# Four RMS norms: the last chunk's squares are added on VectorE before the partition sums, and one more chunk of products goes first in two of them

## The reference

```python
def rmsnorm(x, g):
    xf = x.astype(F32)
    y = xf * lax.rsqrt(jnp.mean(xf * xf, axis=-1, keepdims=True) + EPS)
    return (y * g.astype(F32)).astype(x.dtype)
...
x = x + g1 * (ox @ mla_w_o[j])
...
x = x + g2 * conv_ffn(modulate(rmsnorm(x, norm_ffn_g[i]), sh2, sc2), *ffn)
...
x = x + merged @ w_out[l]
...
return _rmsnorm(x, final_norm_g)
```

## Time and profile before

| | us |
|---|---|
| median of 3 runs | 1647.57 |
| lowest, highest | 1644.97, 1647.64 |
| the profiled execution, span | 1645.5 |

### The profile page before, as it was taken

One profiled execution on the slowest core, in us unless ns is written; L12 is line 12 of the kernel. 1 busy time (PEld: TensorE's weight loads), 2 busy tenths in 40 slices (PEclk: granted clock), 3 DMA queues, 4 the chain that ended last, 5 costly groups with the idle time before them and its releaser, 6 DMA issues.

```text
span 1645.5 us, 24018 instructions
## 1 busy us (share of the span) xinstructions
PE 1633.9 (99%) x8950; PEld 1364.2 (83%) x8950; DVE 1043.6 (63%) x1537; ACT 571.0 (35%) x1017; POOL 1026.5 (62%) x656
## 2 busy tenths in 40 slices
PE   9999999999999999999999999999999999999998
PEld 7887778798888888889887798888888898888887
DVE  3567777677877865635487566655558359746173
ACT  3467777633233232203344243222222121123111
POOL 3455766656666766575579456666676645567663
PEclk9999999999999999999999999999999999999999
DMA  9234335232269863435322233344434253223332
GB/s 371 87 90 129 111 106 165 79 93 96 89 211 320 298 225 103 141 137 172 120 90 65 77 99 102 125 156 140 153 106 143 97 214 120 65 84 103 91 101 90
DMA packets 59095, 220.61 MB, mean 134 GB/s; under 512 B 6849, under 2 KB 9153, under 8 KB 55682
## 3 DMA queue, kind: packets, MB, share of 16 engines
q1 hardware_dynamic: 53826, 204.96, 38.2%
q10 hardware_dynamic: 5184, 14.49, 2.3%
HBM read 201.07 MB, written 14.16 MB: 131 GB/s over the span
## 4 chain that ended last, share of the span: by engine, by line
PE 95%; DVE 4%; ACT 0%; issue 0%; DMA 0%; DVEq 0%; SPq 0%; ACTq 0%
PE PS L2444 28%; PE PS L2446 28%; PE PS L2445 28%; PE PS L2821 3%; PE PS L2783 2%; PE PS L1012 1%; PE PS L2430 1%; PE PS L1785 1%; PE PS L2595 1%; DVE SC L3572 0%; DVE WA L1990 0%; PE PS L1791 0%; DVE MR L3522 0%; PE PS L2720 0%; PE PS L2721 0%
## 5 line engine op out<-in xcount | busy, mean ns | idle before, releaser
L2354 POOL TENSOR_TENSOR WL<-RAW,WH 128x1024 fp32r<-128x1024 f32 (+3 forms) x211 | 542.8, 2572 | 17.6
L2444 PE MATMUL PS<-HH,WH 128*128 128x512 f32 (+1 forms) x1340 | 507.5, 379 | 0.0
L2446 PE MATMUL PS<-HH,WL 128*128 128x512 f32 (+1 forms) x1340 | 502.9, 375 | 0.0
L2445 PE MATMUL PS<-HL,WH 128*128 128x512 f32 (+1 forms) x1340 | 502.9, 375 | 0.0
L2351 POOL TENSOR_SCALAR WH<-RAW 128x1024 fp32r<-128x1024 f32 (+3 forms) x211 | 239.4, 1134 | 287.8 <-PE PS L2446 276.5
L2444 PEld LDWEIGHTS PS<-HH,WH 128*128 128x128 f32 x1340 | 252.2, 188 | 50.7 <-issue 6.2
L2446 PEld LDWEIGHTS PS<-HH,WL 128*128 128x128 f32 x1340 | 252.2, 188 | 45.9
L2445 PEld LDWEIGHTS PS<-HL,WH 128*128 128x128 f32 x1340 | 252.3, 188 | 43.9
L2379 POOL TENSOR_SCALAR PR<-PR,SC 128x768 f32<-128x768 f32 x47 | 107.3, 2292 | 66.7 <-DVE SC L3579 66.3
L2444 PE MATMUL PS<-HIDH,WH 128*128 128x512 f32 (+1 forms) x396 | 145.3, 367 | 0.0
L2445 PE MATMUL PS<-HIDL,WH 128*128 128x512 f32 (+1 forms) x396 | 144.8, 366 | 0.0
(11 more groups left out here) (532 smaller groups left out, 2894.6 us busy)
## 6 DMA issues: line engine op xcount, KB each, us to landing
RAW<-in_wup SPq DMA_DIRECT2D x88, 512.0 KB, 3.6
MRF<-in_modw SPq DMA_DIRECT2D x52, 512.0 KB, 4.8
RAW<-in_wdn SPq DMA_DIRECT2D x32, 704.0 KB, 4.1
MR<-in_modw SPq DMA_DIRECT2D x28, 512.0 KB, 3.6
RAW<-in_whin SPq DMA_DIRECT2D x24, 512.0 KB, 3.5
MK<-in_modk SPq DMA_DIRECT2D x8, 1024.0 KB, 10.9
RAW<-in_wo SPq DMA_DIRECT2D x8, 512.0 KB, 4.2
hy_hs<-HST ACTq DMA_DIRECT2D x4, 1024.0 KB, 4.0
```

The source lines that it names most:

```text
L2354: pool.tensor_tensor(WL[s][:, 0:n], raw[:, 0:n], WH[s][:, 0:n].bitcast(F32), ALU.subtract).then_inc(tile_split, 1)
L2444: pe.matmul(out, wh, xh, start=first, stop=False)
L2445: pe.matmul(out, wh, xl, start=False, stop=False)
L2446: return pe.matmul(out, wl, xh, start=False, stop=last)
```

## The change

In the norms `ffn0`, `hy`, `ffn1` and `n2` VectorE adds the squares of chunk 7 to the running sum (`last_add`, half by half; `n2` has two additions a half), and TensorE sums only SSQ (and SSQ2) over the partitions, behind one wait on `sq_add` in place of the waits on `radd` and `rsq`. `last_add(0)` stands ahead of `half_scale(name, 0)`, `last_add(1)` behind `scaled(2, 0)`. In `ffn0` and `ffn1` the last chunk of tile 6 half 1 goes ahead of the sum, with its `tile_done`. `fin2` stays as it was.

```diff
@@ -2473,19 +2473,21 @@
             def stat_half(name, h):
 
                 n = HALVES[name][1]
-                pe.wait_ge(S["radd"], 7 * n + 6 + h)
-                pe.wait_ge(S["rsq"], 10 * n + 8 + 2 * h)
+                if name == "fin2":
+                    pe.wait_ge(S["radd"], 7 * n + 6 + h)
+                    pe.wait_ge(S["rsq"], 10 * n + 8 + 2 * h)
+                    terms = (SSQ, SQ[1])
+                else:
+                    pe.wait_ge(S["sq_add"], 2 + 2 * n + h)
+                    terms = (SSQ,)
                 for b in (2 * h, 2 * h + 1):
                     r = slice(P * b, P * b + P)
-                    pe.matmul(PS[:, 4, b:b + 1], SSQ[:, r], ONES[:, 0:1], start=True, stop=False)
-                    m = pe.matmul(PS[:, 4, b:b + 1], SQ[1][:, r], ONES[:, 0:1], start=False, stop=True)
+                    for term in terms:
+                        m = pe.matmul(PS[:, 4, b:b + 1], term[:, r], ONES[:, 0:1], start=term is SSQ, stop=term is terms[-1])
                 if name == "n2":
-                    pe.wait_ge(S["radd2"], 6)
-                    pe.wait_ge(S["rsq2"], 8 + h)
                     for b in (2 * h, 2 * h + 1):
                         r = slice(P * b, P * b + P)
-                        pe.matmul(PS[:, 4, 4 + b:5 + b], SSQ2[:, r], ONES[:, 0:1], start=True, stop=False)
-                        m = pe.matmul(PS[:, 4, 4 + b:5 + b], SQ2[1][:, r], ONES[:, 0:1], start=False, stop=True)
+                        m = pe.matmul(PS[:, 4, 4 + b:5 + b], SSQ2[:, r], ONES[:, 0:1], start=True, stop=True)
                 m.then_inc(S["hstat"], 1)
 
             LAST_AT = {2: PS[:, 4, 2:3], 3: PS[:, 5, 2:3]}
@@ -2531,7 +2533,10 @@
                     pe.wait_ge(S["resid"], RBASE[stage] + 6)
                     pe.wait_ge(tile_split, tile_at(stage, 7) + 1)
                     part(7, 0, 0, 0, kn).then_inc(S["half"], 1)
-                    part(6, 0, 1, late, kn - 1)
+                    if name == "fin2":
+                        part(6, 0, 1, late, kn - 1)
+                    else:
+                        part(6, 0, 1, late, kn).then_inc(tile_done, 1)
                 else:
                     pe.wait_ge(S["resid"], RBASE[stage] + 6)
                     pe.wait_ge(tile_split, tile_at(stage, 7, 2, 0) + 1)
@@ -2542,7 +2547,7 @@
                     part(7, 1, 0, 0, kn).then_inc(S["half"], 2)
                     part(7, 0, 1, late, kn).then_inc(tile_done, 1)
                 stat_half(name, 0)
-                if tiles == 1:
+                if name == "fin2":
                     part(6, 0, 1, kn - 1, kn).then_inc(tile_done, 1)
                 ready = {"ffn0": 3, "hy": 4, "ffn1": 3, "n2": 6, "fin2": 3}[name]
                 part(7, tiles - 1, 1, 0, ready)
@@ -3762,6 +3767,17 @@
                                                        ALU.subtract)
                     ins.then_inc(S["hnl"], 1)
 
+                def last_add(h):
+                    dve.wait_ge(S["rsq"], 10 * n + 8 + 2 * h)
+                    dve.wait_ge(S["radd"], 7 * n + 6 + h)
+                    ins = dve.tensor_tensor(SSQ[:, tok(h)], SSQ[:, tok(h)], SQ[1][:, tok(h)], ALU.add)
+                    if name == "n2":
+                        dve.wait_ge(S["rsq2"], 8 + h)
+                        dve.wait_ge(S["radd2"], 6)
+                        ins = dve.tensor_tensor(SSQ2[:, tok(h)], SSQ2[:, tok(h)], SQ2[1][:, tok(h)], ALU.add)
+                    ins.then_inc(S["sq_add"], 1)
+
+                last_add(0)
                 half_scale(name, 0)
                 if name in SPLIT:
                     middle()
@@ -3775,6 +3791,8 @@
                     if k >= 4:
                         low(k - 2, 0)
                     scaled(k, 0)
+                    if k == 2:
+                        last_add(1)
                     if k == 5:
                         half_scale(name, 1)
                 for k in range(2):
```

## The result

The changed kernel takes 1649.2 us (median of 18 runs), the one before 1647.0 in the same session; the ratio is 1.0019 with a 95% interval of 1.0012 to 1.0025, so 3.1 us slower (2.0 to 4.1), just inside 0.2%. The forecast was +2.4. The fastest executions of each, 1647.4 and 1644.6, are 2.8 apart. The profiled execution has a span of 1649.5 us, 4.0 more than that of before.

What follows compares the result with a forecast made beforehand. TensorE, busy 99%, bounds the kernel, but VectorE sets the pace at k=2 to 4 of the norms. -0.2 (`ffn0`, `ffn1`) + 0.2 (`hy`) + 2.35 (`n2`) = +2.4 us on 1647.57 gives 1649.9 us, range 1646.8 to 1654.6.

Steps and rivals of the forecast that it cites:

- TensorE's side: In the four norms, 4.5 us of matmuls removed over two halves; wins before k=4 count only if `low(4)` comes earlier.
- The additions: Ten VectorE additions of 128x256 in the four norms, 0.42 us each, with bounds 0.35 and 0.70.
- `ffn0`, `ffn1`: In these two norms the second addition starts 0.13 us ahead of L2354; `low(2)` 0.1 us earlier in each, together -0.2 us.
- `hy`: In this norm the first half gains 0.15 us, L2354 is 0.08 behind the second addition, and `low(2)` is 0.2 us later.
- The order of start: Where VectorE additions with two SBUF inputs meet GpSimd's L2354, whoever starts first keeps the pair; the other waits the whole instruction.
- `n2`: In this norm's second half L2354 gets between two additions; the second ends at 1333.37, `low(2)` and k=4 2.35 us later.
- the prediction's own sign: Wrong if the nine other additions are not all short, or any norm's k=4 moves over 0.3 us from forecast.
- More collisions: Rival: additions in `hy`, both `ffn` or all three also lose to L2354, 2.25 us each: 1652.2, 1654.4 or 1656.7; chance 0.2.
- No collision in `n2`: Rival: VectorE keeps its place with a second instruction behind the first; sum +0.2, 1647.8 us; chance 0.1.
- The faster side: Rival: TensorE does not wait for VectorE at k=2 to 4, removed 4.5 us count fully: 1643.1; chance 0.1 with partial forms.
- same: Whole kernel's time stays within 0.2% (3.3 us) of the kernel before; chance 0.55.
- slower: Whole kernel ends slower than the kernel before by more than 0.2% (3.3 us); chance 0.37.

Runs made afterwards that it cites:

- experiment 5: Kernel before with chunk 7's squares left out of the sums of four norms, no VectorE addition: 1644.1 us against 1646.5, ratio 0.9990.
- experiment 7: Changed kernel with each norm's second addition one step later on VectorE, behind `scaled(3, 0)`: 1659.5 us against 1646.5 for the kernel before, ratio 1.0080.
- experiment 3: Changed kernel with `n2`'s second running sum finished in a PSUM bank and read from there: 1646.6 us against 1647.3 for the kernel before, ratio 0.9997.
- experiment 4: Changed kernel with 12 unread float32 products filling TensorE's wait before `n2`'s second sum: 1648.2 us against 1647.3 for the kernel before, ratio 1.0009.
- experiment 2: The change in `n2` only, other norms as in the kernel before: 1649.1 us against 1647.3 for the kernel before, ratio 1.0016.
- 9: The changed kernel measured and profiled again, unaltered: 1651.6 us against 1646.1 for the kernel before, ratio 1.0033, from 7 runs.

## Why the prediction was right

**TensorE's side.** Right. The sum in `ffn0` takes 0.37 us for its four matmuls, as against 0.36 forecast, and the spread comes 0.46 earlier, as against 0.45; and it was right not to add the 4.5 us up: experiment 5 gives 2.2 of them, all in the first halves.

**The additions.** 0.42 us forecast, 0.42 to 0.43 measured in all that did not collide. The bounds of 0.35 and 0.70 were wider than needed: the row of the same width decides.

**`ffn0`, `ffn1`.** Forecast -0.2 for the two; -0.15 and -0.09. The residual that no longer waits for tile 6 started at 353.03, as forecast, `scaled(0, 0)` at 354.32 instead of 354.34, the addition 0.16 us ahead of L2354 instead of 0.13. GpSimd's L2354 was to be 0.2 to 0.4 us longer where it came second; it was 0.1 longer in `ffn0` and 0.2 in `hy` (2.57 against 2.38).

**`hy`.** Forecast +0.2, measured +0.25: +0.33 from the first spread to the second, less 0.08 that the first spread gained. The gain was to be 0.15; a sum that TensorE waited for takes 0.47 us (745.58 to 746.05) and not 0.40.

**The order of start.** This was the step on which everything hung, and it held: the second-half additions of `ffn0`, `hy` and `ffn1` and the first of the two in `n2`, ahead by 0.08 to 0.16 us, took 0.42 to 0.43 us; moved behind L2354 (experiment 7) the same four took 2.55 to 2.56; with a PSUM operand (3) the collision disappeared. And the second addition of `n2` lost its place although it stood directly behind the first. The section "Who interferes with whom" of the Trainium skill's "SBUF — State Buffer" says the same of the two SBUF inputs, and the trace agrees in each case (2.51 against 0.42 us).

**`n2`.** The collision and its size were right: the addition was to end at 1333.37 and ended at 1333.44, `low(2)` was to be 2.35 late and was 2.44 late; with the clock held up (experiment 4) `n2` lost 2.4. What the sum lacked is a term: TensorE's clock after the wait. It was worth 1.3 us up to the spread of half 1 in the profiled execution and some 0.2 where the low stretch was short (2.77 against 2.55, experiments 2 and 9). By the prediction's own sign this was a miss: no k=4 was to move by more than 0.3 us from the forecast, and that of `n2` moved by 3.22 us and not 2.35. The wait was also put in the wrong place, at k=2 to 4; it stood in front of the second sum, 2.66 us, and in the first profile there was none for `low(4)`. That the time still came out close, 3.1 us against 2.4, owes something to luck: how much the clock adds differs from run to run, and the one profiled execution lost 4.0. A wait of this length follows from the working (the second addition was to end at 1333.37, and TensorE was at this sum by 1330.81 before), and the Trainium skill, "TensorE: Matmul & The Clock Gate", section "HAM oscillation — how this bites in real kernels", says that waits between bursts of matmuls can put the array back to half rate, so that what follows starts slow. Here that is what rows show: 0.50 behind the wait, 1.00 when the wait was filled. The prediction should have carried the clock as a term of its own, of 0.2 to 1.3 us by these runs.

**The rivals.** More collisions: none, at margins of 0.08 to 0.16 us, in either profile of the changed kernel. No collision in `n2`: refuted. The faster side: refuted by experiment 5. The result, 1.0019 with an interval of 1.0012 to 1.0025, lies on the line between "same" (0.55) and "slower" (0.37), so it cannot tell those two chances apart.

## What to carry to other kernels

Work taken off the busiest engine is worth what it lets the next wait end earlier: here half of the removed matmuls stood in front of a wait for VectorE and were worth nothing. An addition of 0.4 us on VectorE is cheap unless it reads both operands from SBUF while GpSimd has a long instruction that reads SBUF too. Put one operand in PSUM, or let the addition start ahead of that instruction, and do not issue two such additions in a row: the waiting GpSimd instruction got in between them. A stall of TensorE has a second price, its clock afterwards. Of the seven stalls of 2.3 to 2.8 us in these profiles six brought a low stretch, of 3.4 or 6.8 us, and one did not; the stalls of 0.6 and 1.0 us in experiment 3 did not either.

## What the runs showed that I had not expected

Executions of one program differ by 2.5 us before the work has well begun. The text ahead of the prediction has the granted clock of the kernel before at its full level over the whole span; that is wrong. Windows of 5 to 20 us, of the kernel before and of the second profile of the changed kernel:

```profile
5.00:20.00 15.00, 14.16 (x107) 12.03 (x105) 6.48 (x12) 6.49 (x10) 4.10 (x5) 0.77 1.02 420
```

```profile
5.00:20.00 15.00, 14.28 (x119) 12.41 (x118) 7.60 (x15) 6.83 (x11) 3.75 (x4) 1.00 1.01 409
```

In the first the clock is low from 12.8 to 19.7 us (and again from 1641.0 us to the end), and the first spread comes at 59.06 us; in the second it is not low in this stretch, and the same spread comes at 56.55. All the profiles fit this: the spread comes at 59.0 to 59.3 us in the seven with a low stretch of 6.8 us here, at 58.0 in experiment 7 with one of 3.4, and at 56.2 to 56.6 in the three with none. That alone is 2.5 us, as much as the collision in `n2`, and more than half of the spread of the times (1644.5 to 1649.1 for the kernel before). It is why the distances inside one execution were needed to see 0.1 us, and why experiment 2's span looked like no loss.
